# A triangular inverse from blocks of 4 instead of 16, and its last doubling applied to the right hand side

## The chip, the cores and the metric

The kernel runs on one core of one Trainium2 chip. The metric is the device time of one execution in microseconds (us). The engines named here are TensorE (PE, matmul; PEld is its weight load), VectorE (DVE), ScalarE (ACT), GpSimd (POOL) and SyncE (SP, which only issues DMAs here). Each works through its own instructions in order and waits for others on semaphores.

## The reference

Three model blocks run one after the other on a sequence of 1024 positions, width 1024, in fp32. The change concerns one part of the second block, a recurrence with 8 heads of 64 channels:

```python
def step(S, inp):
    r_t, w_t, k_t, v_t, a_t, b_t = inp
    sa = jnp.einsum('bhvk,bhk->bhv', S, a_t)
    S = S * w_t[:, :, None, :] + sa[..., :, None] * b_t[:, :, None, :] + v_t[..., :, None] * k_t[:, :, None, :]
    y = jnp.einsum('bhvk,bhk->bhv', S, r_t)
    return S, y
```

Its output is normalised over each head's 64 channels (mean, variance), scaled, given a bonus term and multiplied with a gate.

## The kernel before, in words

The recurrence is computed in 8 chunks of 128 positions (t = 0 to 7). Within a chunk the rank one updates depend on each other through a strictly triangular 128x128 matrix N for each head; the kernel builds X, the inverse of I minus N, and multiplies the right hand side with it. The 8 heads are handled as two groups b = 0, 1 of four (128x512 tiles, one 128x128 block c for each head).

A chunk is 22 steps on TensorE (`STEPS`, `step`). A step is 8 matmuls, four into one PSUM bank for each b; banks alternate with the step, so step j needs the bank that step j - 2 wrote to be emptied. Steps 0 to 4 are the scores (`SCORES`): D, Nt, Nk, Rb, Rk, products of features over 64 rows. VectorE masks them out of PSUM (`vector_step`); step 0's mask keeps what lies within blocks of 16, step 1 gives both Dt (VectorE) and the whole Nt (ScalarE). Steps 5 to 21 are the solve (`SOLVE`): inverses of blocks of 16 by powers (P2, P2t, P4, P4t, P8t and three additions X += ...), then three doublings to 32, 64 and 128, each a transpose Xt of X, a product Y of a masked part of N (M0, M1, M2) with X, and the addition X += Xt Y. ScalarE copies Xt and Y from PSUM, VectorE adds to X. GpSimd forms the initial X (`begin`) and M0 to M2 (`levels`).

When the inverse of chunk t - 1 is there, `right_side` (its right hand side, after step 21), `unknowns` (X times it, u), `outputs` (state update and y), `means` and `variances` follow, placed between the steps of chunk t. ScalarE takes the results (`take_right_side`, `take_unknowns`, `take_outputs`), VectorE updates the state (`renew`), centres and normalises y, ScalarE takes squares, Ln and Exp of the variance and applies the affine part (`affine`), GpSimd completes y with bonus and gate (`complete`).

In chunks 0 to 5 VectorE and ScalarE also prepare features for two chunks later (m = t + 2): `scale_now`, `shift` (six fused operations), `accumulate` (a scan), `keys`, `square`, `norms`, `clip`, `decays`, `logs`, `inverse_norms`, `directions`, `received`, `given`, `bonus_sums`, `give_bonus`. Chunks 6 and 7 have no m.

GpSimd spends the rest of its time on a convolution of 31 taps (two operations a tap, 128x1024 each); every fourth tap it does `complete(t - 2)`, `begin(t)` and `levels(t)`. Where each piece stands between the steps is written out by hand in the loops of `rwkv`.

Of the kernel before, what the change touches and what calls it, by code (L numbers as in the profile page):

```python
# [2238 lines left out]
STEPS = 22  # L2239


class ChannelParameters:
# [18 lines left out]
    def of(self, name):  # L2261
# [6 lines left out]
SOLVE = [("P2", "Dt", "D"), ("P2t", "D", "Dt"), ("X", "P2t", "X"),  # L2268
# [5 lines left out]

BY_VECTOR = {0: 1, 1: 2, 2: 3, 3: 4, 4: 5, 5: 6, 7: 7, 8: 8, 10: 9, 11: 10, 12: 11, 15: 12, 18: 13, 21: 14}
BY_SCALAR = {1: 1, 6: 2, 9: 3, 13: 4, 14: 5, 16: 6, 17: 7, 19: 8, 20: 9}
PER_VECTOR, PER_SCALAR = 14, 9

NEEDS = [(0, 0), (0, 0), (1, 0), (2, 1), (3, 0),
         (4, 0), (5, 0), (6, 2), (6, 2), (7, 2), (8, 3), (8, 3), (10, 3), (11, 3), (11, 3), (11, 5),  # L2280
         (12, 5), (12, 5), (12, 7), (13, 7), (13, 7), (13, 9)]


class Recurrence:


    def __init__(self, core, st, par, arena):
        sb = st.sb
        self.core, self.sig, self.par = core, st.sem, par
        self.mask = {n: sb(n, [P, P]) for n in ("mask_lt", "tri", "mask16", "mask16T", "level0", "level1", "level2")}  # L2290
# [9 lines left out]
        self.m = {n: tile(n) for n in ("D", "Dt", "Nt", "P2", "P2t", "Nk", "M0", "M1", "M2")}  # L2300
        self.m |= {"P4": self.m["D"], "P4t": self.m["Dt"], "P8t": self.m["P2t"], "Xt": self.m["Nt"], "Y": self.m["P2"]}
# [41 lines left out]
    def step(self, pe, t, j):  # L2343
# [4 lines left out]
        for b in range(2):  # L2348
            if j == 0 and t:
                self.after_scalar(pe, t - 1, b, 20)  # L2350
            if j == 1 and t:
                self.after_vector(pe, t - 1, b, 21)
# [5 lines left out]
            if j == 7:  # L2358
                pe.wait_ge(self.sig(f"begun{b}"), t + 1)
            if j == 14:  # L2360
                pe.wait_ge(self.sig(f"masked{b}"), t + 1)
        if j < 5:
            _, l, r = SCORES[j]
            for c in range(4):
                for b in range(2):
                    rows = slice(64 * b, 64 * b + 64)
                    mm = nc.tensor.matmul(core.acc[2 * b + j % 2][:, c * P:(c + 1) * P], self.chunk(l, t)[rows, c, :],
# [5 lines left out]
        for b in range(2):  # L2373
            for c in range(4):
                cs = slice(c * P, (c + 1) * P)
                to = core.acc[2 * b + j % 2][:, cs]
# [46 lines left out]

    def outputs(self, pe, t):
# [3 lines left out]
        pe.wait_ge(self.sig("u"), t + 1)  # L2428
# [50 lines left out]
    def scalar_step(self, a, t, j):  # L2479
# [3 lines left out]
        for b in range(2):  # L2483
# [321 lines left out]
def rwkv(core, par, x):  # L2805

    nc, d = core.nc, core.d
    with Stage(core, "rwkv") as st:
# [10 lines left out]
        with nc.Block() as block:  # L2819
# [66 lines left out]
            def _(pe):  # L2886
# [6 lines left out]
                for t in range(NT):  # L2893
# [3 lines left out]
                    for j in range(STEPS):  # L2897
# [5 lines left out]
                        if j == 3 and t:  # L2903
                            w.outputs(pe, t - 1)
# [1399 lines left out]
```

## Time and profile before

| | |
|---|---|
| median of 3 runs | 4715.8 us (4712.62 to 4719.29) |
| profiled execution, its own time | 4716.23 us |
| its span in the trace | 4714.5 us |
| TensorE busy | 4271.3 us (91%) |
| VectorE, ScalarE, GpSimd busy | 1893.1, 1342.0, 1140.6 us |
| one middle chunk, window 1743 to 1800 us: TensorE, VectorE, ScalarE, GpSimd busy | 50.66, 38.25, 27.76, 34.48 us |
| granted clock of the whole execution | 0.95 |

Times in the trace count from the start of the span. A timeline row gives the start, the duration of a run of equal instructions, the engine and line, what is written and read, how many there are, and in brackets the idle time before it and who ended it. Each fp32 matmul leaves two records, so a step of 8 matmuls is x16. A row's duration contains the drain of its last instruction; the distance of two starts is what a piece costs. Names drop indices: `rwkv_P_sb` is P2 or P4 or Y in the same buffer, `rwkv_Dt_sb` may hold P4t, `rwkv_Nt_sb` may hold Xt, `x_here` is the buffer that the features lie in.

### The profile page before, as it was taken

Reading aid. Unit: us, or ns where it says so; the run is one execution under the profiler, and the core shown is the slowest. Engines: PE = TensorE matmul, PEld = TensorE weight load, DVE = VectorE, ACT = ScalarE, POOL = GpSimd, SP = SyncE. Lnnn points to the kernel's source line nnn. Section 1 sums busy time; section 2 is a strip of 40 time slices with the busy share of each in tenths; the row PEclk is TensorE's granted clock in tenths of the full one; section 3 lists DMA queues with packets and bytes.
Section 4 is the critical chain, followed back from the end, with each engine's and each line's share of the span. In section 5 each row is a group of like instructions: output and inputs, shape, how many; then the busy total and the mean of one; then the engine's idle time right before and its main releaser. Section 6 shows DMA issues by size and latency. Waiting matters only on the chain. (4 is left out here: it accounts for less than half of the span.)

```text
span 4714.5 us, 55607 instructions
## 1 busy us (share of the span) xinstructions
PE 4271.3 (91%) x21558; PEld 3505.4 (74%) x21558; DVE 1893.1 (40%) x3298; ACT 1342.0 (28%) x2358; POOL 1140.6 (24%) x555
## 2 busy tenths in 40 slices
PE   8998797877996888689999999999999999977897
PEld 6887675766674888567888886888788888856676
DVE  3021565671487665255235334000033333346433
ACT  3120232341322444322000103112243444443112
POOL 2220001052152666222222221221111111122323
PEclk9998898978997999899999999999999999978899
DMA  3233101041442110121111112332333334266422
GB/s 123 101 143 91 33 17 43 22 139 45 156 148 97 39 41 19 51 100 45 45 54 45 49 41 78 121 135 86 104 94 92 93 109 109 61 208 191 163 78 92
DMA packets 279789, 413.05 MB, mean 88 GB/s; under 512 B 53109, under 2 KB 188150, under 8 KB 273658
## 3 DMA queue, kind: packets, MB, share of 16 engines
q1 hardware_dynamic: 224250, 310.02, 21.4%
q10 hardware_dynamic: 53104, 94.92, 5.4%
q0 software_dynamic: 2192, 4.80, 0.4%
q8 instruction: 162, 2.65, 0.2%
q14 instruction: 81, 0.66, 0.0%
HBM read 286.18 MB, written 123.47 MB: 87 GB/s over the span
## 5 line engine op out<-in xcount | busy, mean ns | idle before, releaser
L163 POOL TENSOR_TENSOR weights_wlow<-weights_raw,weights_whigh 128x1024 fp32r<-128x1024 f32 (+1 forms) x236 | 695.9, 2970 | 2444.5 <-ACT weights_whigh L154 2444.5
L154 ACT ACTIVATE weights_whigh<-weights_raw 128x1024 fp32r<-128x1024 f32 (+1 forms) x236 | 266.2, 1162 | 1176.5 <-PE acc L313 791.0
L313 PE MATMUL acc<-h_high_half,weights_whigh 128*128 128x512 f32 x1408 | 553.7, 393 | 25.0 <-POOL weights_wlow L163 21.2
L313 PE MATMUL acc<-h_high_half,weights_wlow 128*128 128x512 f32 x1408 | 550.4, 391 | 0.0
L313 PE MATMUL acc<-h_low_half,weights_whigh 128*128 128x512 f32 x1408 | 550.4, 391 | 0.0
L313 PEld LDWEIGHTS acc<-h_high_half,weights_whigh 128*128 128x128 f32 x1408 | 265.9, 189 | 89.8 <-POOL weights_wlow L163 22.5
L3524 PE MATMUL acc<-h_high_half,weights_whigh 128*128 128x512 f32 x768 | 331.3, 431 | 0.0
L313 PEld LDWEIGHTS acc<-h_low_half,weights_whigh 128*128 128x128 f32 x1408 | 265.9, 189 | 55.8
L313 PEld LDWEIGHTS acc<-h_high_half,weights_wlow 128*128 128x128 f32 x1408 | 265.9, 189 | 55.7 <-issue 1.0
L3524 PE MATMUL acc<-h_low_half,weights_whigh 128*128 128x512 f32 x768 | 302.2, 393 | 0.0
L3524 PE MATMUL acc<-h_high_half,weights_wlow 128*128 128x512 f32 x768 | 300.8, 392 | 0.0
L316 PE MATMUL acc<-weights_wlow,h_high_half 128*128 128x512 f32 x768 | 298.8, 389 | 0.0
L316 PE MATMUL acc<-weights_whigh,h_low_half 128*128 128x512 f32 x768 | 298.8, 389 | 0.0
L316 PE MATMUL acc<-weights_whigh,h_high_half 128*128 128x512 f32 x768 | 298.8, 389 | 0.0
L313 PE MATMUL acc<-y_high_half,weights_whigh 128*128 128x512 f32 x448 | 182.5, 407 | 30.4 <-DVE x_here L4087 19.8
L1972 DVE TENSOR_TENSOR x_here<-x_here,acc 128x512 f32<-128x512 f32 x80 | 54.9, 687 | 371.8 <-PE acc L313 371.8
L313 PE MATMUL acc<-hidden_high,weights_wlow 128*128 128x512 f32 x512 | 199.2, 389 | 0.0
L313 PE MATMUL acc<-hidden_high,weights_whigh 128*128 128x512 f32 x512 | 199.2, 389 | 0.0
L3432 DVE SCALAR_TENSOR_TENSOR gated_biased_sb<-gated_near_ends_sb,gated_slope_sb,acc 128x384 f32<-128x384 f32 x40 | 24.5, 614 | 413.2 <-DMA gated_end_sb<-rows 271.8
L313 PE MATMUL acc<-y_high_half,weights_wlow 128*128 128x512 f32 x448 | 179.6, 401 | 0.0
L313 PE MATMUL acc<-y_low_half,weights_whigh 128*128 128x512 f32 x448 | 179.3, 400 | 0.0
L3524 PEld LDWEIGHTS acc<-h_high_half,weights_whigh 128*128 128x128 f32 x768 | 145.8, 190 | 31.1
(536 smaller groups left out, 8174.2 us busy)
## 6 DMA issues: line engine op xcount, KB each, us to landing
weights_raw<-w_cols SPq DMA_DIRECT2D x94, 512.0 KB, 5.0
weights_raw<-w_ff SPq DMA_DIRECT2D x64, 512.0 KB, 3.8
weights_raw<-w_rows SPq DMA_DIRECT2D x30, 1024.0 KB, 7.1
att<-gated_result_sb SPq DMA_DIRECT2D x96, 130.0 KB, 2.2
merge_o_sb<-att SPq DMA_DIRECT2D x24, 520.0 KB, 6.7
rows<-norm_square ACTq DMA_DIRECT2D x48, 256.0 KB, 2.1
weights_raw<-w_out SPq DMA_DIRECT2D x24, 512.0 KB, 3.8
cols<-first_out ACTq DMA_DIRECT2D x40, 256.0 KB, 2.0
```

The source lines that it names most:

```text
L154: self.core.nc.scalar.activation(high[p][:, half * (KC // 2):(half + 1) * (KC // 2), :], raw[half], ACT.Copy).then_inc(self.core.sem("roun ...
L163: self.core.nc.gpsimd.tensor_tensor(low[p][:, hs, :], raw[half], high[p][:, hs, :].bitcast(F32), ALU.subtract).then_inc(self.core.sem("wei ...
L313: mm = nc.tensor.matmul(core.acc[b][:, :], wt[p][:, k, c * P:(c + 1) * P], h[:, k, half * HALF:(half + 1) * HALF], start=first, stop=final)
L316: mm = nc.tensor.matmul(core.acc[b][:, 0:width], h[:, k, b * P:(b + 1) * P], wt[p][:, k, :], start=first, stop=final)
L1972: return core.nc.vector.tensor_tensor(to, to, acc, ALU.add)
L3432: nc.vector.scalar_tensor_tensor(out=biased, in0=mask, scalar=self.slope[p][:, st["dilation"]:st["dilation"] + 1], in1=acc, op0=ALU.mult, ...
L3524: mm = nc.tensor.matmul(core.acc[b][:, :], wt[n % 2][:, k, c * P:(c + 1) * P], of[:, k, half * HALF:(half + 1) * HALF], start=(k == 0 and ...
```

## The change

Blocks of 4 are inverted by powers, which needs one square only (P2t) and one addition. Four doublings follow in place of three, to 8, 16, 32 and 64. So X holds the inverses of the two 64x64 diagonal blocks. The last doubling is applied to the right hand side: u's first half is X times the first 64 rows, a product with the off-diagonal block (`across`, copied out of step 0's bank by VectorE) is added to the second 64 rows (`raise_second`), and `unknowns` runs a second time for u's second half. Steps become 19. The order of the surrounding pieces on each engine changes too: `outputs` stand behind step 9 instead of 3, `means` behind 12, `variances` behind 15, `bonus_sums` behind 17; ScalarE has Ln and root of the variance apart from those of the norms, behind step 17; `levels` has a fourth mask M3 that waits for step 6.

```diff
-STEPS = 22
+STEPS = 19
-SOLVE = [("P2", "Dt", "D"), ("P2t", "D", "Dt"), ("X", "P2t", "X"),
-         ("P4", "P2t", "P2"), ("P4t", "P2", "P2t"), ("X", "P4t", "X"),
-         ("P8t", "P4", "P4t"), ("X", "P8t", "X"),
-         ("Xt", None, "X"), ("Y", "M0", "X"), ("X", "Xt", "Y"),
-         ("Xt", None, "X"), ("Y", "M1", "X"), ("X", "Xt", "Y"),
-         ("Xt", None, "X"), ("Y", "M2", "X"), ("X", "Xt", "Y")]
+SOLVE = [("P2t", "D", "Dt"), ("X", "P2t", "X")] + [
+    step for i in range(4) for step in (("Xt", None, "X"), ("Y", f"M{i}", "X"), ("X", "Xt", "Y"))]
...
-    def unknowns(self, pe, t):
+    def unknowns(self, pe, t, i):
-        pe.wait_ge(self.sig("rhs"), t + 1)
-        for b in range(2):
-            self.after_vector(pe, t, b, 21)
+        if i:
+            pe.wait_ge(self.sig("second"), t + 1)
+        else:
+            pe.wait_ge(self.sig("rhs"), t + 1)
+            for b in range(2):
+                self.after_vector(pe, t, b, 18)
...
+    def second_half(self, pe, t):
+
+        nc, core = self.core.nc, self.core
+        across = self.across[t % 2][:, :, :].rearrange("p i t -> p (i t)")
+        pe.wait_ge(self.sig("u"), 2 * t + 1)
+        for c in range(4):
+            for b in range(2):
+                e = slice(c * P + b * HD, c * P + (b + 1) * HD)
+                at = 4 * b + c
+                mm = nc.tensor.matmul(core.acc[4][:, e], across[:, at * HD:(at + 2) * HD], self.u[0:HD, e],
+                                      start=True, stop=True)
+        mm.then_inc(self.sig("second_sum"), 1)
...
+                if j == 0:
+                    ins.then_inc(self.sig(f"by_vector{b}"), 1)
+                    ins = nc.vector.tensor_copy(self.across[t % 2][:, 1 + 4 * b:5 + 4 * b, :], self.four(acc)[0:HD, :, HD:])
...
+    def raise_second(self, v, t):
+
+        second = self.rhs[HD:, :]
+        v.wait_ge(self.sig("rhs"), t + 1)
+        v.wait_ge(self.sig("second_sum"), t + 1)
+        self.core.nc.vector.tensor_tensor(second, second, self.core.acc[4][HD:, :], ALU.add).then_inc(self.sig("second"), 1)
...
+        for i in range(4):
+            for b in range(2):
+                if i == 0:
+                    self.after_scalar(pool, t, b, 1)
+                if i == 3:
+                    pool.wait_ge(self.sig(f"step{b}"), STEPS * t + 7)
...
                         w.step(pe, t, j)
                         if j == 1 and t:
-                            w.unknowns(pe, t - 1)
+                            w.unknowns(pe, t - 1, 0)
                         if j == 2:
                             w.turn(pe, t, 0)
                         if j == 3 and t:
-                            w.outputs(pe, t - 1)
+                            w.second_half(pe, t - 1)
...
                         if j == 6 and t:
+                            w.unknowns(pe, t - 1, 1)
+                        if j == 9 and t:
+                            w.outputs(pe, t - 1)
+                        if j == 12 and t:
                             w.means(pe, t - 1)
-                        if j == 8 and t:
+                        if j == 15 and t:
                             w.variances(pe, t - 1)
-                        if j == 18 and m:
+                        if j == 17 and m:
                             w.bonus_sums(pe, m)
                 w.right_side(pe, NT - 1)
-                w.unknowns(pe, NT - 1)
+                w.unknowns(pe, NT - 1, 0)
+                w.second_half(pe, NT - 1)
+                w.unknowns(pe, NT - 1, 1)
                 w.outputs(pe, NT - 1)
```

On TensorE, in front of the solve of a middle chunk, before: the last two products of `outputs`, score 4, a turn, step 5, a turn, the norms:

```order
3646 L2439 MATMUL acc<-rwkv_Rb_1_sb,rwkv_rhs_sb 64x128
3647 L2440 MATMUL acc<-rwkv_Rk_1_sb,rwkv_rows_sb 64x128
3648 L2367 MATMUL acc<-x_here 128x128 x8
3649 L2394 MATMUL acc<-ident_here,x_here 128x128 x4
3650 L2380 MATMUL acc<-rwkv_D_sb,rwkv_Dt_sb 128x128 x8
3651 L2394 MATMUL acc<-ident_here,rwkv_V_sb 128x128 x4
3652 L2452 MATMUL acc<-rwkv_sq_sb,rwkv_block_mean_sb 128x256 x2
```

The same place after the change, from score 3 to step 6 and the start of the second pass of the unknowns:

```order
3616 L2367 MATMUL acc<-x_here 128x128 x8
3617 L2436 MATMUL acc<-rwkv_rhs_sb,rwkv_across_sb 128x64 x8
3618 L2367 MATMUL acc<-x_here 128x128 x8
3619 L2394 MATMUL acc<-ident_here,x_here 128x128 x4
3620 L2380 MATMUL acc<-rwkv_Dt_sb,rwkv_D_sb 128x128 x8
3621 L2394 MATMUL acc<-ident_here,rwkv_V_sb 128x128 x4
3622 L2468 MATMUL acc<-rwkv_sq_sb,rwkv_block_mean_sb 128x256 x2
3623 L2380 MATMUL acc<-rwkv_X_0_sb,rwkv_P2t_sb 128x128 x4
3624 L2380 MATMUL acc<-rwkv_X_1_sb,rwkv_P2t_sb 128x128 x4
3625 L2424 MATMUL acc<-rwkv_rhs_sb,rwkv_X_0_sb 128x64
```

The 28 matmuls of `outputs` have left the place ahead of score 4 and eight products with across stand there.

On VectorE, the start of a middle chunk after the change (before it, the two masks D stood together and there was no copy to across):

```order
1238 L2620 TENSOR_TENSOR rwkv_D_sb<-acc,rwkv_mask_sb 128x512
1239 L2623 COPY rwkv_across_sb<-acc 64x256
1240 L2620 TENSOR_TENSOR rwkv_D_sb<-acc,rwkv_mask_sb 128x512
1241 L2623 COPY rwkv_across_sb<-acc 64x256
1242 L2620 TENSOR_TENSOR rwkv_Dt_sb<-acc,rwkv_mask4T_sb 128x512 x2
```

The rest of the chunk's front has the same operations in the same order up to Rk; behind it stands `raise_second`, ahead of the key product.

On ScalarE, the end of a chunk after the change: the last copies of Xt and Y, then what leads to the right side of the chunk:

```order
702 L2503 ACTIVATE rwkv_Dt_sb<-acc 128x512 x2
703 L2503 ACTIVATE rwkv_D_sb<-acc 128x512 x2
704 L2587 ACT_TABLE_LOAD
705 L2587 ACTIVATE rwkv_ysq_sb<-acc,rwkv_eps_sb 128x512
706 L2592 ACT_TABLE_LOAD
707 L2592 ACTIVATE rwkv_ysq_sb<-rwkv_ysq_sb 128x512
708 L2605 ACTIVATE rwkv_y_sb<-rwkv_y_sb,channel_parameters 128x128 x4
709 L2513 ACTIVATE rwkv_rhs_sb<-acc 128x512
```

Before, the copy of the right side (L2499) came directly behind the last copies of Y (L2489), and Ln, root and affine stood earlier in the chunk.

## Rows read from the trace of the kernel before

**Rows 1.** Timeline, TensorE: start, duration, line, operands; chunks 1, 4, 6, 7 start.

```profile
1571.60 2.06 PE L2367 MATMUL acc<-x_here 64*128 64x128 f32 x32
...
1742.30 2.06 PE L2367 MATMUL acc<-x_here 64*128 64x128 f32 x32
...
1856.10 2.06 PE L2367 MATMUL acc<-x_here 64*128 64x128 f32 x32
...
1911.77 2.06 PE L2367 MATMUL acc<-x_here 64*128 64x128 f32 x32
```

**Rows 2.** Timeline, TensorE, chunk 4 from the outputs on.

```profile
1748.98 0.49 PE L2431 MATMUL acc<-rwkv_rhs_sb,rwkv_rows_sb 128*128 128x128 f32 x2
...
1754.82 1.16 PE L2367 MATMUL acc<-x_here 64*128 64x128 f32 x16
...
1756.69 2.02 PE L2380 MATMUL acc<-rwkv_D_sb,rwkv_Dt_sb 128*128 128x128 f32 x16
...
1759.85 1.95 PE L2380 MATMUL acc<-rwkv_Dt_sb,rwkv_D_sb 128*128 128x128 f32 x16
...
1777.72 1.06 PE L2378 MATMUL acc<-ident_here,rwkv_X_sb 128*128 128x128 f32 x8 [0.98 <-DVE rwkv_X_sb L2611]
1778.62 1.95 PE L2380 MATMUL acc<-rwkv_X_sb,rwkv_M_sb 128*128 128x128 f32 x16
1781.35 2.02 PE L2380 MATMUL acc<-rwkv_P_sb,rwkv_Nt_sb 128*128 128x128 f32 x16 [0.78 <-ACT rwkv_P_sb L2489]
1784.35 1.06 PE L2378 MATMUL acc<-ident_here,rwkv_X_sb 128*128 128x128 f32 x8 [0.98 <-DVE rwkv_X_sb L2611]
```

**Rows 3.** Timeline, VectorE, the first half of chunk 4.

```profile
1743.49 1.29 DVE L2605 TENSOR_TENSOR rwkv_D_sb<-acc,rwkv_mask_sb 128x512 f32<-128x512 f32 x2 [3.03 <-PE acc L2367]
...
1749.81 1.27 DVE L2605 TENSOR_TENSOR rwkv_Nk_sb<-acc,rwkv_mask_lt_sb 128x512 f32<-128x512 f32 x2
...
1755.27 1.27 DVE L2605 TENSOR_TENSOR rwkv_Rb_sb<-acc,rwkv_tri_sb 128x512 f32<-128x512 f32 x2
...
1759.06 1.87 DVE L2660 TENSOR_TENSOR rwkv_kx_sb<-rwkv_kx_sb,rwkv_k_sb 128x512 f32<-128x512 f32 x1
...
1767.21 0.84 DVE L2624 TENSOR_TENSOR rwkv_S_sb<-rwkv_S_sb,acc 64x256 f32<-64x256 f32 x2
```

**Rows 4.** Timeline, GpSimd, the level masks of chunk 4.

```profile
1746.72 8.34 POOL L2746 TENSOR_TENSOR rwkv_M_sb<-rwkv_Nt_sb,rwkv_level_sb 128x512 f32<-128x512 f32 x6
```

**Rows 5.** Timeline, TensorE, the front of chunk 0.

```profile
1522.86 2.08 PE L2367 MATMUL acc<-x_here 64*128 64x128 f32 x16 [3.21 <-DVE rwkv_Nk_sb L2605]
...
1528.31 2.74 PE L2380 MATMUL acc<-rwkv_D_sb,rwkv_Dt_sb 128*128 128x128 f32 x16 [2.32 <-DVE rwkv_Rb_sb L2605]
...
1533.12 1.95 PE L2380 MATMUL acc<-rwkv_Dt_sb,rwkv_D_sb 128*128 128x128 f32 x16
```

**Rows 6.** Window of chunk 0: us, TensorE busy (records), granted clock, DMA share, GB/s.

```profile
1530.00:1531.00 1.00, 1.00 (x6) 0.50 0.00 0
```

**Rows 7.** Timeline, ScalarE: a decay in chunk 4; Ln, root, affine in the tail.

```profile
1764.15 0.39 ACT L2553 ACTIVATE rwkv_up_sb<-rwkv_C_sb,rwkv_middle_sb 128x128 f32<-128x128 f32 x1
...
1982.17 0.69 ACT L2572 ACTIVATE rwkv_ysq_sb<-acc,rwkv_eps_sb 128x512 f32<-128x512 f32 x1 [0.87 <-PE acc L2474]
1982.88 1.28 ACT L2577 ACT_TABLE_LOAD   x1
...
1985.56 1.65 ACT L2590 ACTIVATE rwkv_y_sb<-rwkv_y_sb,channel_parameters 128x128 f32<-128x128 f32 x4 [0.76 <-DVE rwkv_y_sb L2730]
```

**Rows 8.** Timeline, TensorE: last X step and start of the last outputs.

```profile
1962.86 2.02 PE L2380 MATMUL acc<-rwkv_P_sb,rwkv_Nt_sb 128*128 128x128 f32 x16 [0.78 <-ACT rwkv_P_sb L2489]
...
1970.88 0.49 PE L2431 MATMUL acc<-rwkv_rhs_sb,rwkv_rows_sb 128*128 128x128 f32 x2 [0.69 <-ACT rwkv_rhs_sb L2504]
```

**Rows 9.** Timeline, GpSimd and VectorE in chunk 0.

```profile
1530.89 2.85 POOL L2865 TENSOR_SCALAR rwkv_term_sb<-rwkv_conv_in_sb,rwkv_ctaps_sb 128x1024 f32<-128x1024 f32 x1
...
1532.11 0.67 DVE L2660 TENSOR_TENSOR rwkv_kx_sb<-rwkv_kx_sb,rwkv_k_sb 128x512 f32<-128x512 f32 x1
```

More of the change, by code:

```diff
@@ L2289, in __init__ @@
         self.core, self.sig, self.par = core, st.sem, par
-        self.mask = {n: sb(n, [P, P]) for n in ("mask_lt", "tri", "mask16", "mask16T", "level0", "level1", "level2")}
+        self.mask = {n: sb(n, [P, P]) for n in ("mask_lt", "tri", "mask4", "mask4T", "level0", "level1", "level2", "level3")}
         self.block_mean, self.keep = sb("block_mean", [P, P]), sb("keep", [P, 2 * QUARTER])
@@ L2299, in __init__ @@
         tile = lambda n: [sb(f"{n}{b}", [P, RW]) for b in range(2)]
-        self.m = {n: tile(n) for n in ("D", "Dt", "Nt", "P2", "P2t", "Nk", "M0", "M1", "M2")}
-        self.m |= {"P4": self.m["D"], "P4t": self.m["Dt"], "P8t": self.m["P2t"], "Xt": self.m["Nt"], "Y": self.m["P2"]}
+        self.m = {n: tile(n) for n in ("D", "Dt", "Nt", "P2t", "Nk", "M0", "M1", "M2")}
+        self.m |= {"Xt": self.m["Dt"], "Y": self.m["D"], "M3": self.m["P2t"]}
+        self.across = [sb(f"across{p}", [HD, 9, HD]) for p in range(2)]
         self.late = {n: [tile(f"{n}{p}_") for p in range(2)] for n in ("Rb", "Rk", "X")}
@@ L2366, in step @@
                     rows = slice(64 * b, 64 * b + 64)
-                    mm = nc.tensor.matmul(core.acc[2 * b + j % 2][:, c * P:(c + 1) * P], self.chunk(l, t)[rows, c, :],
+                    mm = nc.tensor.matmul(self.bank(t, j, b)[:, c * P:(c + 1) * P], self.chunk(l, t)[rows, c, :],
                                           self.chunk(r, t)[rows, c, :], start=True, stop=True)
@@ L2375, in step @@
                 cs = slice(c * P, (c + 1) * P)
[L2376 removed]
+                to = self.bank(t, j, b)[:, cs]
                 if l is None:
@@ L2741, in levels @@
     def levels(self, pool, t):
-        for b in range(2):
-            self.after_scalar(pool, t, b, 1)
-            for i in range(3):
-                ins = self.core.nc.gpsimd.tensor_tensor(self.four(self.tile(f"M{i}", t, b)), self.four(self.tile("Nt", t, b)),
-                                                        self.spread(self.mask[f"level{i}"]), ALU.mult)
-            ins.then_inc(self.sig(f"masked{b}"), 1)
+        for i in range(4):
[4 more added lines that the diff above has]
+                    pool.wait_ge(self.sig(f"step{b}"), STEPS * t + 7)
+                self.core.nc.gpsimd.tensor_tensor(self.four(self.tile(f"M{i}", t, b)), self.four(self.tile("Nt", t, b)),
+                                                  self.spread(self.mask[f"level{i}"]), ALU.mult).then_inc(self.sig(f"begun{b}"), 1)
     def complete(self, pool, f):
@@ L2967, in _ @@
                             w.take_rows(a, t, 2)
-                        if j == 7:
-                            if t:
-                                w.centre_squares(a, t - 1)
-                            if m:
-                                w.decays(a, m, 0)
+                        if j == 6 and t:
+                            w.take_unknowns(a, t - 1, 1)
+                        if j == 7 and m:
+                            w.decays(a, m, 0)
                         if j == 8 and m:
                             w.decays(a, m, 1)
-                        if j == 10:
+                        if j == 9:
                             if m:
                                 w.logs(a, m)
-                            if t:
-                                w.log_variance(a, t - 1)
-                            if m:
                                 w.inverse_norms(a, m)
-                            if t:
-                                w.root(a, t - 1)
+                        if j == 10 and t:
+                            w.take_outputs(a, t - 1)
+                        if j == 14 and t:
+                            w.centre_squares(a, t - 1)
+                        if j == 17 and t:
+                            w.log_variance(a, t - 1)
+                            w.root(a, t - 1)
                         if j == 18 and t:
@@ L2999, in _ @@
                 nc.vector.memset(w.eps[:, :], 64e-5)
+                for p in range(2):
+                    nc.vector.memset(w.across[p][:, 0, :], 0.0)
                 nc.vector.memset(w.S[:, :, :], 0.0).then_inc(sig("state"), 1)
```

97 lines of the change are left out of this document (49 added, 48 removed).

## The prediction, made before the changed kernel ran

> **What bounds the kernel now.** The windows of the page show TensorE as the busy engine everywhere, so the question is what sets the time of one stage, the recurrence (1513 to 1990 us). It works through 8 chunks, and the starts of a chunk on TensorE give its period [rows 1]: 56.90 us for each of the middle chunks 1 to 5 (two of them lie between 1742.30 and 1856.10), 55.67 for chunk 6, and chunk 1 starts at 1571.60. I call the time since a chunk's first score its place. TensorE is in order and nearly full: in a middle chunk it waits seven times, always in the solve, for 0.78 us (a ScalarE copy) or 0.98 us (a VectorE add or copy), 6.1 us in all [rows 2]. What is easily missed is the second engine. From place 1.2 (1743.49) to place 18.6 (1759.06 plus 1.87) VectorE does not pause: masks, six fused shifts, a scan, key product [rows 3]. The second three shifts fill 4.26 us from the end of the two Nk masks (1749.81 plus 1.20) to Rb (1755.27), 1.42 each, as long as one of GpSimd's six mask operations beside them (8.34 for six, 1.39 each): one shift gets in behind each of them [rows 3, 4]. TensorE has 5.84 us of outputs between scores 3 and 4 (1748.98 to 1754.82) and arrives at step 5 (1756.69) just as the mask Rb is done (1755.27 plus 1.27), so VectorE costs nothing there.
>
> **Part 1, the solve.** Four full product steps go (P2, P4, P4t, P8t); two of three power additions go too, and one doubling (transpose, Y, X) comes. A step is 1.86 us without a wait, a transpose 0.90 (1777.72 to 1778.62), from Y to X it is 2.73 (1.95 work, 0.78 wait), from X to the next transpose 3.0 [rows 2]. Work: 22 steps with 14 products in the solve become 19 with 10, so -4 x 1.86 + 0.90 = -6.5 us a chunk.
>
> **Part 2, the split right side.** Each chunk adds a second pass of 8 unknown products and 8 products with across. Neither is short for having 64 columns or 64 rows: weights of 128 columns are loaded for each, and all across products use the same 64 rows, so I take a step's 1.9 us for each, bounds 1.16 (the score at 1754.82, which runs its two row halves together) and 2.0 [rows 2]. Together +3.8. In the loop these passes lie in waits of others; TensorE pays their work only.
>
> **Part 3, VectorE in front.** Two copies of 64x256 are new before Dt. The nearest row is the state addition, 0.84 for two [rows 3]: +0.8 us. Outputs leave the place between scores 3 and 4; only the across products (1.9) stand there. Now TensorE is early. By places: scores 0, 1 and the first unknowns to 4.1, score 2, turn, score 3 to 6.9, across to 8.8; score 4 needs Nk, done at 8.8 now (1749.81 plus 1.27) and at 9.6 with the copies, hence 11.4 with the turn. Step 5 needs Rb, done at 14.2 now [rows 3] and at 15.0 then. GpSimd starts its masks some 2 us later than today, as it now completes an older chunk's output at the chunk's start; each shift still meets one of its operations, and I take the shifts at today's 1.42. **TensorE waits some 3.8 us there.** Step 5, a turn and the norms, 3.16 us now (1756.69 to 1759.85), put step 6 at 18.3 [rows 2].
>
> **Part 4, fillers.** Unknowns, outputs, means, variances now stand behind X steps and bonus behind Y, and use up the 0.98 and 0.78 waits (with a filler of 0.9 an X step still takes 3.0). At step 9 a price appears: ScalarE has half of the decays, four operations of 0.39 and two small ones that overlap [rows 7], between the copy of the transpose and that of Y: +0.6 us. Adding up from step 6 at 18.3: unknowns to 22.1, transpose and Y to step 9 at 26.4, outputs to 34.1, three doublings (0.9 + 2.73 + 3.0 twice, the last one 0.9 + 2.8 + 1.86) to 52.9, right side 2.7: period 55.6 at full clock, **1.3 us less than now**. Chunk 1 has no older chunk to complete, so GpSimd lets VectorE go earlier: 1.2 more.
>
> **Part 5, the clock.** Chunk 0 shows what a wait in front does: TensorE waits 3.21 us for Nk, then 2.32 for Rb, the granted clock falls to 0.50, the 1.2 GHz level, and step 5 to step 6 takes 4.81 us (1528.31 to 1533.12) where the full clock takes 3.16 [rows 2, 5, 6]. A wait of 3.8 us in every middle chunk should do the same: +1.6 us each, bounds 0 (the clock holds) and 2.8 (scores and step 6 too). Middle chunks: 5 x 1.3 + 1.2 - 5 x 1.6 = -0.3 us gained. So the recurrence gets nothing where VectorE has its preparation to do.
>
> **Part 6, chunks without preparation (6 and 7) and chunk 0.** Here VectorE has no shifts. Places: score 4 at 8.7, step 5 at 10.4, step 6 at 13.1, unknowns, transposes at 16.9, step 9 at 20.5 (no decays), outputs to 28.3, step 18 at 45.1 to 47.0, right side: 49.7. Against 55.67 that is 5.95 each, **11.9 us**. Chunk 0 has no unknowns and keeps its front: the shifts end with GpSimd's operations, so the 0.8 of copies is absorbed and step 5 stays at 1528.3. Afterwards 6 at 1533.1, 9 at 40.4, 12 at 47.4 (table loads delay two copies), 18 at 61.0, next chunk at 1565.6: **6.0 us**.
>
> **Part 7, the tail.** Nothing covers the split solve after the last chunk. Before, the last X step starts at 1962.86, ends at 1964.72, and outputs start 6.16 us later [rows 8]. After, ScalarE still has the previous chunk's Ln, root and affine in its queue before it takes the right side: load 1.28, Ln 0.7, load 1.28, and up to the affine's end 3.05 more (1984.16 to 1987.21), 6.3 us behind the last Y copy [rows 7]. The right side is then taken at 4.85 behind the X step, unknowns 2.0, half copy 0.65, across 2.0, addition 0.8, unknowns 2.0, copy 0.7: outputs at 13.05, **-6.9 us**, and 0.7 for the chance that the 2.2 us wait lowers the clock.
>
> **Sum.** 6.0 - 0.3 + 11.9 - 7.6 = 10.0 us off the profiled execution's 4716.2 (span 4714.5 plus 1.7), which is 0.4 above the median: 4705.8. The following stages wait for the end of this one, and take the gain whole.
>
> **GpSimd** needs a word of its own: one more level mask is two operations of 1.39 [rows 4], and its wait for step 6 adds idle time; busy 34.5 us of a chunk today, it will be busy some 37 of 55.6 or 49.7; the last mask M3 is ready by place 22, needed at 48. Nobody waits for it.
>
> **Rivals.** *The clock holds* (the wait is under 3.8, or split otherwise): the 8.0 and the 0.7 come back, 18.7 us, 4697.1. For it: the seven short waits of today leave the clock at 1.00. Against: chunk 0's 2.32 was enough. 17%.
>
> *The front is worse than laid out* (a shift misses a gap of GpSimd, 1.4 us, or the clock stays down to 2.8): 1 to 1.4 us more in each of 5 chunks, 3 to 5 us gained in all, 4711 to 4713. 17%.
>
> *GpSimd holds VectorE up in the middle, slower than before.* Directions, rates, renewal and the received features move into places 31 to 38, while GpSimd works on the taps; today these six run behind the taps. Should each wait for a GpSimd operation, the group takes 2 x 1.42 + 4 x 1.87 = 10.3 us instead of 6 x 0.67 = 4.0 at most, step 12's addition starts at 42.2 instead of 38.8, and the given features cost 1 more: 4.5 in 6 chunks, 27 us, so 4733. It decides once the group exceeds the roughly 7 us between inverse norms (31.3) and that addition. Against it: a key product took 0.67 in chunk 0 at 1532.11 in the middle of a GpSimd tensor_scalar (1530.89, 2.85 long), while one behind a GpSimd tensor_tensor took 1.87 [rows 9]. Only one tap operation in two holds it back, and the slack takes that. 8%. The Trainium skill (SBUF — State Buffer, section "Who interferes with whom") states that a VectorE instruction with two SBUF inputs contends with any GpSimd instruction that reads SBUF; by that rule the time would be this rival's, and the row at 1532.11 speaks against it.
>
> **How the numbers follow.** Forecast 58% (own range 4701 to 4711: across products at 1.1 give 5 more, clock cost 0.8 to 2.4 gives 4 either way). Range 4696 to 4715: it takes in the clock that holds and most of the worse front, and leaves out the slower rival. About 0.2%, 9.4 us, is what a measurement of this kernel tells from no change, and the forecast lies at that edge: faster by over 0.2% takes 0.17 and just over half of 0.58, 0.50; slower 0.08; the rest, 0.42, within.
>
> **What would show it.** Periods in the profile after: near 57 for chunks 2 to 5, 50 for 6, 52.6 for 0. A TensorE wait for Rb of 3 to 4 us per middle chunk, a granted clock below 1.00 behind it, shifts of 1.4 as today. Outputs 13 us behind the last X step. A middle period under 55 says the clock or the front was misread; a wait of step 13 or 16 for X over 1.5 us says it is GpSimd. A changed time outside the stage would make all of it wrong.

## The result, and the profile after

The changed kernel takes 4685.3 us (median; 4683.4 to 4691.9), the kernel before 4715.2 in the same comparison: a ratio of 0.9938, 95% interval 0.9921 to 0.9956, so 29.9 us less. The forecast was 4705.8 with a range down to 4696. The sign is right, the gain is three times what I gave, and the time lies outside the range. The profiled execution of after is the longest of its four (4691.9, span 4690.2), the others lie 6.5 to 8.5 us lower; the first experiment bears on why.

The stage by chunk, windows of the profiled execution, each from one first score matmul to the next, the last up to 1933. Columns: window and length, then busy time (records) of PE, PEld, DVE, ACT and POOL, the granted clock, DMA share, GB/s.

```profile
1512.50:1568.50 56.00, 40.71 (x318) 37.50 (x317) 34.40 (x44) 23.29 (x47) 35.61 (x19) 0.88 0.20 59
1568.50:1626.06 57.56, 48.69 (x426) 43.95 (x425) 38.19 (x50) 29.98 (x57) 34.80 (x18) 0.97 0.12 36
1626.06:1683.58 57.52, 48.78 (x426) 43.83 (x425) 39.78 (x51) 31.50 (x61) 37.57 (x20) 0.97 0.15 42
1683.58:1733.68 50.10, 46.64 (x425) 42.22 (x424) 32.98 (x51) 31.38 (x61) 40.91 (x20) 1.00 0.17 49
1733.68:1783.80 50.12, 46.66 (x426) 42.23 (x425) 33.01 (x51) 31.39 (x61) 40.91 (x20) 1.00 0.08 22
...
1833.91:1883.11 49.20, 45.25 (x418) 40.90 (x417) 18.22 (x30) 21.20 (x37) 35.47 (x20) 1.00 0.08 22
```

Before, every middle chunk took 56.90 [rows 1]. After, there are two kinds of them and nothing between: chunks 1 and 2 take 57.5, chunks 3, 4 and 5 take 50.1. The work is the same (425 or 426 matmul records in each). VectorE is busy 39.8 in one and 33.0 in the other, and GpSimd, the other way round, 37.6 and 40.9. I call them **held** and **free** chunks, after what happens to VectorE.

TensorE in a held chunk (2) and in a free one (4), in the timeline: start, us, engine, line, operation; in brackets the idle time before it and who ended it. First step 5 and step 6 of chunk 2:

```profile
1640.40 2.53 PE L2380 MATMUL acc<-rwkv_Dt_sb,rwkv_D_sb 128*128 128x128 f32 x16 [3.70 <-DVE rwkv_Rb_sb L2620]
1645.23 1.95 PE L2380 MATMUL acc<-rwkv_X_sb,rwkv_P2t_sb 128*128 128x128 f32 x16
```

and of chunk 4, with the product Y of step 9:

```profile
1743.72 1.95 PE L2380 MATMUL acc<-rwkv_Dt_sb,rwkv_D_sb 128*128 128x128 f32 x16
...
1746.81 1.95 PE L2380 MATMUL acc<-rwkv_X_sb,rwkv_P2t_sb 128*128 128x128 f32 x16
...
1754.69 2.02 PE L2380 MATMUL acc<-rwkv_D_sb,rwkv_Dt_sb 128*128 128x128 f32 x16 [1.54 <-ACT rwkv_D_sb L2503]
```

The held chunk is the one I forecast: 3.70 us of waiting for Rb (3.8 in Part 3), then step 5 to step 6 in 4.83 instead of 3.09, at a granted clock of 0.50 between 1642 and 1645, of which one window (columns as above):

```profile
1643.00:1644.00 1.00, 1.00 (x5) 0.92 (x4) 0.97 (x3) 0.75 (x2) 0.00 (x0) 0.50 0.00 0
```

The free chunk has no wait for Rb at all; step 6 stands at place 13.1 instead of 19.2. The cause stands on VectorE, here again chunk 2 and then chunk 4:

```profile
1630.31 0.47 DVE L2661 SCALAR_TENSOR_TENSOR rwkv_r_sb<-rwkv_raw_sb,channel_parameters,rwkv_r_sb 128x256 f32<-128x256 f32 x1
1630.70 1.49 DVE L2661 SCALAR_TENSOR_TENSOR rwkv_k_sb<-rwkv_raw_sb,channel_parameters,rwkv_k_sb 128x256 f32<-128x256 f32 x1
...
1738.34 0.47 DVE L2661 SCALAR_TENSOR_TENSOR rwkv_k_sb<-rwkv_raw_sb,channel_parameters,rwkv_k_sb 128x256 f32<-128x256 f32 x1
1738.73 0.47 DVE L2661 SCALAR_TENSOR_TENSOR rwkv_V_sb<-rwkv_raw_sb,channel_parameters,rwkv_V_sb 128x256 f32<-128x256 f32 x1
```

and on GpSimd, chunk 2 and chunk 4 (the initial X, two operations):

```profile
1630.37 2.96 POOL L2761 TENSOR_TENSOR rwkv_X_sb<-rwkv_D_sb,ident_here 128x512 f32<-128x512 f32 x2
...
1737.98 4.75 POOL L2761 TENSOR_TENSOR rwkv_X_sb<-rwkv_D_sb,ident_here 128x512 f32<-128x512 f32 x2
```

From the second shift on, a shift takes 0.47 us in the free chunk and 1.49 in the held one; in the free chunk it is GpSimd that needs 4.75 us for its two operations, which take 2.51 in chunk 1:

```profile
1570.46 2.51 POOL L2761 TENSOR_TENSOR rwkv_X_sb<-rwkv_D_sb,ident_here 128x512 f32<-128x512 f32 x2 [11.47 <-DVE rwkv_D_sb L2620]
```

In both chunks the first shift starts at place 4.25, ahead of GpSimd's operation, and takes 0.47; GpSimd's operation comes 0.06 us later in the held chunk and 0.04 in the free one. So the chunks part not at the first shift but at the second. Before, GpSimd's initial X was under way when the first shift came, in each chunk (in chunk 4 from place 1.96 to 4.47, the shift at 3.59). After, from chunk 2 on, it completes an older output first, at the start of the chunk, and the two meet.

The tail: ScalarE, then the three passes of the split solve and the outputs on TensorE.

```profile
1932.26 1.66 ACT L2605 ACTIVATE rwkv_y_sb<-rwkv_y_sb,channel_parameters 128x128 f32<-128x128 f32 x4 [0.76 <-DVE rwkv_y_sb L2753]
1933.82 0.57 ACT L2513 ACTIVATE rwkv_rhs_sb<-acc 128x512 f32<-128x512 f32 x1
```

```profile
1927.69 2.02 PE L2380 MATMUL acc<-rwkv_D_sb,rwkv_Dt_sb 128*128 128x128 f32 x16 [0.78 <-ACT rwkv_D_sb L2503]
1934.44 2.93 PE L2424 MATMUL acc<-rwkv_rhs_sb,rwkv_X_sb 128*128 128x64 f32 x16 [2.10 <-ACT rwkv_rhs_sb L2513]
1938.05 3.67 PE L2436 MATMUL acc<-rwkv_rhs_sb,rwkv_across_sb 64*128 64x64 f32 x16 [0.68 <-ACT rwkv_rhs_sb L2519]
1942.58 3.68 PE L2424 MATMUL acc<-rwkv_rhs_sb,rwkv_X_sb 128*128 128x64 f32 x16 [0.85 <-DVE rwkv_rhs_sb L2637]
1946.93 0.80 PE L2447 MATMUL acc<-rwkv_rhs_sb,rwkv_rows_sb 128*128 128x128 f32 x2 [0.68 <-ACT rwkv_rhs_sb L2519]
```

The last output is stored at 1967.95 where it was 1989.91. **Where the 21.96 us of the stage come from**, chunk by chunk against before: start 0.43; chunk 0 58.64 - 55.97 = 2.67; chunks 1 and 2 -0.66 and -0.62; chunks 3 to 5 6.8 each, 20.4; chunk 6 6.47; chunk 7 with the tail 78.14 - 84.84 = -6.70. Another 2.3 of the span's 24.3 lie in later stages, spread over many waits; single executions of the kernel before differ by more (4712.6 to 4719.3).

### The profile page after: what moved, and what is told of

Read it like the earlier page. It is cut to its first block and busy times, and to the rows that moved or that the text cites. A ratio compares the mean times of both kernels' runs of the same rounds, so it can differ in the third digit from the quotient of the medians.

```text
span 4690.2 us, 55196 instructions
## 1 busy us (share of the span) xinstructions
PE 4257.3 (91%) x21366; PEld 3493.4 (74%) x21366; DVE 1868.5 (40%) x3260; ACT 1366.5 (29%) x2392; POOL 1172.8 (25%) x571
```

## The experiments

All edits are to the changed kernel unless said. The starts of the chunks in each profiled execution give the periods that the verdicts rest on; for the overview first the table, worked out from the first score matmul of each chunk in the timelines (no chunk follows chunk 7; "7 + tail" is from its start to the next stage's load of the finished rows):

| kernel | ch 0 | 1 | 2 | 3 | 4 | 5 | 6 | 7 + tail |
|---|---|---|---|---|---|---|---|---|
| before | 58.6 | 56.9 | 56.9 | 56.9 | 56.9 | 56.9 | 55.7 | 84.6 |
| after | 56.0 | 57.6 | 57.5 | 50.1 | 50.1 | 50.1 | 49.2 | 91.3 |
| after, once more | 56.4 | 57.5 | 50.1 | 50.2 | 50.1 | 50.1 | 49.2 | 91.1 |
| GpSimd behind all six shifts | 46.1 | 51.2 | 51.2 | 51.2 | 51.1 | 51.2 | 49.2 | 91.6 |
| GpSimd ahead of the shifts | 56.2 | 57.5 | 57.6 | 57.6 | 57.6 | 58.4 | 49.2 | 91.3 |
| before, GpSimd behind the shifts | 52.3 | 56.5 | 56.5 | 56.5 | 56.5 | 56.6 | 55.7 | 83.6 |
| GpSimd behind the first shift | 52.2 | 56.9 | 50.1 | 50.1 | 50.1 | 50.1 | 49.2 | 90.1 |
| and the tail's order | 46.1 | 51.2 | 51.2 | 51.2 | 51.2 | 51.2 | 49.2 | 87.1 |
| and decays earlier | 45.8 | 51.2 | 51.2 | 51.2 | 51.2 | 51.2 | 49.2 | 91.3 |
| and unsplit | 53.9 | 57.3 | 58.8 | 57.3 | 58.8 | 57.4 | 56.9 | 83.0 |
| and unsplit, logarithm later | 54.1 | 55.7 | 55.9 | 55.9 | 55.9 | 55.9 | 53.7 | 86.3 |
| all that helped | 45.8 | 49.7 | 49.7 | 49.7 | 49.7 | 49.7 | 49.2 | 88.8 |

The lines that begin with "and" are edits on top of "GpSimd behind all six shifts".

**The same kernel once more.**

> The kernel after, unchanged. Theory A (a race for the memory port): whether a middle chunk has a period of 50.1 or 57.5 us is decided by which of two operations starts first at place 4.3, the first shift on VectorE or GpSimd's initial X, and they lie 0.04 to 0.06 us apart. So the number of chunks with 50.1 differs from one execution to the next, with no period in between, and the times lie in steps of about 7.4 us: 4684.6 (one slow chunk less than in the profile) or 4691.9. Rival B (the first chunks are slow for a reason of their own, such as the loads still under way): chunks 1 and 2 are slow and 3 to 5 fast in every execution.

4683.8 us (4680.9 to 4690.0, 4 runs), ratio 0.9927 [0.9911, 0.9944]. Chunk 2, held in the first profile, is free in this one. Windows of chunks 1 and 2, columns as above:

```profile
1568.89:1626.41 57.52, 48.66 (x425) 43.99 (x424) 38.19 (x50) 29.82 (x57) 34.78 (x18) 0.97 0.12 36
1626.41:1676.50 50.09, 46.66 (x425) 42.23 (x424) 33.03 (x51) 31.34 (x61) 40.91 (x20) 1.00 0.17 48
```

and GpSimd's initial X of that chunk, whose first shift starts at 1630.67:

```profile
1630.70 4.75 POOL L2761 TENSOR_TENSOR rwkv_X_sb<-rwkv_D_sb,ident_here 128x512 f32<-128x512 f32 x2
```

It comes 0.03 us behind the shift here, 0.06 in the first profile. Theory A holds for chunk 2 in what matters, same program, same chunk, 7.4 us apart, with no period between; its wording does not, since the first shift starts ahead of GpSimd in both. Rival B keeps a part: chunk 1 is held in both, for a steady reason. It has no older output to complete, so GpSimd starts its initial X at 1570.46 in the first profile, well ahead of the first shift (1572.76). The executions of after, 4691.9 and 4690.0 on one side, 4680.9 to 4685.4 on the other, fit one chunk more or less being held, though only two of them have a profile.

**GpSimd's initial X behind the shifts.** In `begin`, for chunks 0 to 5:

```diff
+        if t + 2 < PAIRS:
+            pool.wait_ge(self.sig("shifted"), 6 * (t + 2) + 6)
         for b in range(2):
             pool.wait_ge(self.sig(f"by_vector{b}"), PER_VECTOR * t + 1)
```

> One wait more on GpSimd: the initial X of chunks 0 to 5 starts only when the six shifts are done. Theory A: the shifts take 0.47 us each in every chunk, chunks 1 to 5 all have periods of 50.1 us, the waits for Nk and Rb in chunk 0 (2.65 and 2.33) go with their clock loss: 4691.9 - 2 x 7.4 - about 6 = 4671 us. Rival B: the order on GpSimd is without effect, chunks 1 and 2 stay at 57.5, 4685 us.

4672.9 us (4668.5 to 4674.0), ratio 0.990 [0.9883, 0.9916]: 11 less than after measured beside it, by a wait and nothing else. Chunk by chunk against the second run of after, chunk 0 gives 10.3 and chunk 1 gives 6.4, the two in which GpSimd was always first; chunks 2 to 5, free in that run, lose 1.0 to 1.1 each. All 36 shifts take 0.46 or 0.47. Chunk 0 loses 10 us rather than the 6 expected, since with the front its 3.16 us wait for X ahead of step 13 and the half clock behind that (step 14 took 3.57) go too. The middle chunks come out at 51.2, not 50.1: GpSimd's work now runs later, and VectorE's group in the middle of the chunk is slower (in chunk 4 the directions take 2.42 us for two and the state's fade 2.73, against 1.45 and 1.72 in the free chunk 4 of after). TensorE waits 1.17 for X ahead of step 13, where a free chunk has no wait. TensorE in chunk 3, the Y of step 9 and the transpose of step 13:

```profile
1681.69 2.02 PE L2380 MATMUL acc<-rwkv_D_sb,rwkv_Dt_sb 128*128 128x128 f32 x16 [1.53 <-ACT rwkv_D_sb L2503]
...
1696.99 1.07 PE L2378 MATMUL acc<-ident_here,rwkv_X_sb 128*128 128x128 f32 x8 [1.17 <-DVE rwkv_X_sb L2629]
```

**GpSimd first.** `w.begin` stands ahead of `w.complete` in GpSimd's loop.

> On GpSimd the initial X stands ahead of the two operations that complete an older output, as it did before at place 2. Theory A: GpSimd is always at work when the first shift comes, the shifts take 1.4 to 1.5 us in all of chunks 0 to 5, every middle period is 57 to 58 us, TensorE waits 3.7 us for Rb, clock 0.50 behind it: 4691.9 + 3 x 7.4 = 4714 us. Rival B: 4685 us, chunks 3 to 5 at 50.

4717.4 us (4714.2 to 4721.6, 10 runs), ratio 0.9998 [0.9988, 1.0007]. Every middle chunk is held, and the whole gain is gone. Chunk 3, window and TensorE's wait ahead of step 5:

```profile
1685.25:1742.80 57.55, 48.76 (x426) 43.93 (x425) 39.84 (x51) 31.45 (x61) 37.37 (x20) 0.97 0.15 42
```

```profile
1699.62 2.92 PE L2380 MATMUL acc<-rwkv_Dt_sb,rwkv_D_sb 128*128 128x128 f32 x16 [3.71 <-DVE rwkv_Rb_sb L2620]
```

The period is close to what the prediction adds up to, 55.6 plus 1.6 for the clock (chunk 5 alone took 58.4). So this kernel is nearest to the one I forecast, except that its tail, chunk 0 and chunk 1 are dearer than I had them.

**The kernel before, with the same wait on GpSimd.**

> The kernel before with the same wait on GpSimd (initial X only behind the six shifts). Theory A: VectorE's front shortens by some 5 us here too, but the outputs between scores 3 and 4 keep TensorE busy until then, so chunks 1 to 5 stay at 56.9 us; only chunk 0, which has no outputs, loses its waits of 3.2 and 2.3 us and 1.6 of clock: 4708 us. If instead the middle periods of the kernel before fall too, VectorE's front bounded that kernel as well. Rival B: 4715 us.

4709.9 us (4702.6 to 4711.6, 10 runs), ratio 0.9978 [0.9969, 0.9988]: 9 us less. Chunk 0 gives 6.4, the middle chunks 0.36 each. With the outputs between scores 3 and 4 a faster front brings the old kernel next to nothing in the loop. The shifts take 0.47 to 0.48 there too, so it is the new order of the fillers that makes the front count, and the free shifts that make it short.

**Behind the first shift only.** The same wait with `+ 1` instead of `+ 6`.

> GpSimd's initial X waits only for the first of the six shifts instead of all six. Theory A1 (who is first keeps the port: VectorE's operations that follow one another without a pause hold GpSimd off until a mask comes that reads PSUM): the shifts stay at 0.47, GpSimd's two operations of the initial X slip into the masks, as in the fast chunks of the kernel after, all middle periods 50.1 instead of 51.17 us of the kernel with the full wait, 4672.9 - 5.3 = 4667.6 us. Rival A2 (the order of starting matters only because GpSimd idles; as soon as it is let in, it holds the later shifts): the second three shifts take 1.4 to 1.5, periods 54 to 57.5, 4690 to 4704 us.

4681.6 us (4679.7 to 4682.1). Neither theory whole: four chunks are free at 50.1, chunk 1 is held at 56.9, chunk 0 takes 52.2. VectorE and GpSimd in chunk 1:

```profile
1570.11 0.47 DVE L2661 SCALAR_TENSOR_TENSOR rwkv_k_sb<-rwkv_raw_sb,channel_parameters,rwkv_k_sb 128x256 f32<-128x256 f32 x1
1570.51 1.49 DVE L2661 SCALAR_TENSOR_TENSOR rwkv_V_sb<-rwkv_raw_sb,channel_parameters,rwkv_V_sb 128x256 f32<-128x256 f32 x1
```

```profile
1570.27 3.11 POOL L2763 TENSOR_TENSOR rwkv_X_sb<-rwkv_D_sb,ident_here 128x512 f32<-128x512 f32 x2 [12.16 <-DVE rwkv_r_sb L2661]
```

GpSimd arrives 0.16 us behind the start of k, waits for k's end, and is let in before V. In chunk 2 it arrives at the same distance (k at 1627.00, GpSimd at 1627.16) and is held off through V, and so in chunks 3 to 5; in chunk 0, 0.22 behind k, it is let in before V. In these rows an operation that is under way keeps its pace; what happens at the boundary to the next one is not decided by the distance alone, and stays open. Of the two waits tried, only the full one frees the shifts in all chunks.

**The tail's order.** In the last chunk the affine step of chunk 6 moves behind `take_unknowns`:

```diff
-                        if j == 18 and t:
+                        if j == 18 and 0 < t < NT - 1:
                             w.affine(a, t - 1)
...
                 w.take_unknowns(a, NT - 1, 1)
+                w.affine(a, NT - 2)
```

> The kernel with the full wait on GpSimd, and in the last chunk ScalarE takes the right side and both halves of the unknowns ahead of the affine step of the chunk before. TensorE's wait of 2.09 us ahead of the last unknowns becomes 0.55. If the clock then stays at full speed, the three passes of the split solve take 2.0, 1.9 and 2.0 instead of 3.44, 3.67 and 3.68 and the outputs start at full speed: 1.5 + 5 + 1.9 = 8.4 us, 4664.5 us. If the clock falls all the same, only the 1.5 us: 4671.4 us.

4667.2 us (4666.4 to 4667.5), 5.7 less than without it, between the two cases. The two were measured in different comparisons; taken each against the kernel before beside it, the difference is 4.7 (50.7 and 46.0).

```profile
1912.29 2.00 PE L2424 MATMUL acc<-rwkv_rhs_sb,rwkv_X_sb 128*128 128x64 f32 x16 [0.69 <-ACT rwkv_rhs_sb L2513]
1914.97 2.00 PE L2436 MATMUL acc<-rwkv_rhs_sb,rwkv_across_sb 64*128 64x64 f32 x16 [0.68 <-ACT rwkv_rhs_sb L2519]
1917.82 3.68 PE L2424 MATMUL acc<-rwkv_rhs_sb,rwkv_X_sb 128*128 128x64 f32 x16 [0.85 <-DVE rwkv_rhs_sb L2637]
```

The wait shrinks by 1.40 (2.09 to 0.69), and two passes that took 3.44 and 3.67 take 2.00 each, 4.5 us together and the whole change of the tail (91.57 to 87.10). The third pass still runs at a clock of 0.50: three waits of 0.69, 0.68 and 0.85 us ahead of it went with that. When the clock falls is not settled by these waits: the last kernel below has the same tail, and there it is down already for the second pass, behind 0.69 and 0.68, and the tail takes 88.8.

**Decays earlier.** ScalarE's first half of the decays moves from step 7 to behind step 5.

> The kernel with the full wait on GpSimd, and the first half of the decays moved from between the transpose's copy and the Y copy (step 7) to the idle time of ScalarE behind step 5. If the price of the decays at step 9 is what the prediction said, TensorE's wait there falls from 1.53 (1.36 in chunk 0) to 0.78 us: 5 x 0.75 + 0.6 = 4.4 us, 4668.5 us. If ScalarE comes late with something else, or VectorE's later timetable bounds the chunk, nothing: 4673 us.

4672.7 us (4669.7 to 4677.7), no change against 4672.9, the periods likewise. TensorE's waits in chunk 3:

```profile
1679.55 2.02 PE L2380 MATMUL acc<-rwkv_D_sb,rwkv_Dt_sb 128*128 128x128 f32 x16 [0.78 <-ACT rwkv_D_sb L2503]
...
1695.63 1.06 PE L2378 MATMUL acc<-ident_here,rwkv_X_sb 128*128 128x128 f32 x8 [1.95 <-DVE rwkv_X_sb L2629]
```

The wait at step 9 went from 1.53 to 0.78 (the prediction priced it at 0.6), and the wait at step 13 from 1.17 to 1.95 took it all back. The wait is for VectorE's addition to X, which stands behind its group of directions, rates, renewal and received features; the last experiment moves that group.

**Without the split.** Five level masks, five doublings (22 steps), the full inverse, one pass of unknowns, no copies of the across block.

> The kernel with the full wait on GpSimd, and the last doubling as a matrix step again: five level masks, five doublings, 22 steps, no copies of the across block, no second half, one pass of unknowns. By the prediction's terms a doubling costs 6.6 us and the split 3.8, so 2.8 more in chunks 1 to 7 and 6.6 more in chunk 0; the tail's outputs start 6.2 instead of 17.9 us behind the last X step: 7 x 2.8 + 6.6 - 11.7 = +14.5, 4687.4 us, with middle periods of 54.0. If the split passes cost less than I took (1.2 each), 5 to 10 us more than that.

4718.9 us (4710.1 to 4722.6, 10 runs), 46 more, three times what I expected. Part of that was my placement: ScalarE's Ln and root, with their table loads, stood in front of the last doubling's copies, and TensorE waited 2.42 there.

> The unsplit kernel once more, with the logarithm, root and affine of the older chunk placed behind the copies of the last doubling instead of in front of them, which cost a wait of 2.42 where others are 0.78 and a fall of the clock in every second chunk (periods 57.3 and 58.8). Expected: periods of chunks 1 to 5 57.3 - 1.6 = 55.7, chunk 7's tail as in the first unsplit kernel, 4718.9 - 7 x 1.6 - 3 x 1.5 = 4703 us. That would put the price of a doubling as a matrix over the split at 55.7 - 51.2 = 4.5 us a chunk in the loop, against 2.8 by the prediction's terms; if it comes to 54.0 the prediction's terms hold.

4703.6 us (4697.7 to 4706.8, 7 runs), ratio 0.9971 [0.996, 0.9982]. With that mended the middle period is 55.9. Against the split at 51.2 the matrix doubling costs 4.7 us a chunk, 4.5 in chunk 6, 8.0 in chunk 0, and gives back 5.2 in chunk 7 with the tail. By the terms of Parts 1 and 2 it should be 2.8 (6.6 less 3.8) in the loop. The other 1.9 are for the most part waits that the split's passes cover: without them TensorE waits 0.64 for Rb, 0.49 for Rk and 0.98 for X behind step 6, 2.1 us, and the split kernel has none of the three. (The account is not exact: the split kernel in turn waits 1.17 at step 13, which this one does not.) In the loop the two passes cost some 1.9 (6.6 less 4.7), not 3.8. In all the split is worth 31 us with this order (4703.6 against 4672.9). The three waits in chunk 4 of the unsplit kernel:

```profile
1740.35 2.02 PE L2379 MATMUL acc<-rwkv_Dt_sb,rwkv_D_sb 128*128 128x128 f32 x16 [0.64 <-DVE rwkv_Rb_sb L2616]
1744.17 2.02 PE L2379 MATMUL acc<-rwkv_X_sb,rwkv_P2t_sb 128*128 128x128 f32 x16 [0.49 <-DVE rwkv_Rk_sb L2616]
1747.17 1.06 PE L2377 MATMUL acc<-ident_here,rwkv_X_sb 128*128 128x128 f32 x8 [0.98 <-DVE rwkv_X_sb L2622]
```

**All that helped in one.** The full wait on GpSimd, the tail's order, the decays, and on VectorE:

```diff
-                        if j == 11:
-                            if t:
-                                w.renew(v, t - 1)
-                            if m:
-                                w.received(v, m)
+                        if j == 10 and m:
+                            w.received(v, m)
...
+                        if j == 15 and t:
+                            w.renew(v, t - 1)
```

> All that helped in one: the full wait on GpSimd, the tail's order on ScalarE, the first half of the decays behind step 5, and on VectorE the received features right behind the directions, the given ones behind step 12 and the state's renewal behind step 15. If VectorE's group of directions, renewal and received features, 9.6 us long beside GpSimd's taps, is what took back the 0.75 us of the decays (a wait for X of 1.95 ahead of step 13), that wait goes and the middle period becomes 50.1 - 0.75 = 49.4 us: 4667.2 - 5 x 1.8 - 0.5 = 4657.7 us. If the wait only moves to step 16 or to the right side, 4664 to 4667 us.

4660.6 us (4659.8 to 4664.8), ratio 0.9878 [0.9861, 0.9894]. The wait at step 13 is gone and 0.43 us remain at step 16; middle chunks take 49.7, 0.3 more than expected. The tail gave less than in the kernel that brought its order (88.8 against 87.1), since the second pass ran at half clock here:

```profile
1907.36 3.67 PE L2436 MATMUL acc<-rwkv_rhs_sb,rwkv_across_sb 64*128 64x64 f32 x16 [0.68 <-ACT rwkv_rhs_sb L2519]
```

The window of chunk 3:

```profile
1656.62:1706.27 49.65, 46.65 (x425) 42.15 (x424) 35.17 (x51) 31.56 (x61) 37.77 (x20) 1.00 0.17 49
```

This version is 58 us faster than the kernel before beside it, against 35 for the change in the comparison of its second run, and all its middle chunks have one period in the one execution profiled.

## Why the prediction was wrong in size

**Part 3, "each shift still meets one of its operations, and I take the shifts at today's 1.42", is the step that failed** ("its" is GpSimd's). It held in chunks 1 and 2 and failed in 3 to 5. I had seen that GpSimd "starts its masks some 2 us later than today", and noted the work that it does first, but did not place that against the shifts. The masks of D and Dt and the copies end at place 4.2; the affine step is done at 1.7, the older output takes GpSimd 2.6 us, and it is free at 4.3. A tie to within 0.1 us has two outcomes, and I priced one. The price of the other: shifts of 0.47, no wait of 3.7, no fall of the clock, and no wait of 1.5 ahead of step 13, so 57.5 - 50.1 = 7.4 us a chunk, 6.0 of them ahead of step 6. Three free chunks are 22 us, more than the forecast's whole gain. The kernel with GpSimd first, where all are held, took the time of the kernel before; with GpSimd behind all six, every shift takes 0.47. How often the tie falls one way no sum of mine could have given: three of the four chunks that meet it were free in one execution and four of four in the other.

The Trainium skill (SBUF — State Buffer, section "Who interferes with whom") says that where VectorE and GpSimd contend for the port pair they share, the one that issues first has it for the whole instruction and the other is blocked (it says so of VectorE's 2-port modes), and that the order of issue decides who blocks. I had drawn on that section for the rule on which operations contend, and not for this one. The rows agree for a single operation: the first shift, under way when GpSimd comes, takes 0.47 in both kinds of chunk, and where GpSimd is let in the shift behind it takes 1.49. The masks, with one input in PSUM, take 1.27 for two in held and free chunks alike. But the order of the starts does not part the two kinds, for VectorE was first in both; what the rows add is that VectorE's operations in close succession can keep GpSimd out over three of them.

**Part 5, the clock: right where its condition held.** Held chunks measured 57.5 where 55.6 + 1.6 = 57.2 was forecast, with 4.83 us from step 5 to step 6 against the 4.81 that I took from chunk 0. That the period is so near is in part luck, two misses that nearly cancel. Step 6 stands at place 19.2 and not at 18.3 + 1.6 = 19.9, because the 0.8 us of the copies is absorbed (the last shift starts at place 11.52 in chunk 2, and at 11.56 in the middle chunks before): I had reasoned so for chunk 0 and not for these. And the rest of the chunk takes 38.4 instead of 37.3, with a wait of 1.48 ahead of step 13 that I did not have. The 1.2 for chunk 1 did not come either: its last shift starts at 11.56. The rival "the clock holds" described the free chunks' clock, for another reason.

**Parts 1, 2 and 4: right, as sums.** From step 6 to the next chunk I had 55.6 - 18.3 = 37.3 us; a free chunk takes 37.0. The wait at step 9 was to be 0.78 + 0.6, it is 1.54. Chunk 6 was to take 49.7 and takes 49.2. The unsplit kernel adds that leaving the two passes out saves less than their 3.8 us of work, because they cover waits that would stand there without them.

**Part 6, chunk 0: 2.7 us instead of 6.0.** The front is as forecast (step 6 at 1532.7, forecast 1533.1). Missing was a wait of 3.16 us for the X of step 12, ahead of step 13, and the half clock that follows it:

```profile
1552.04 1.06 PE L2378 MATMUL acc<-ident_here,rwkv_X_sb 128*128 128x128 f32 x8 [3.16 <-DVE rwkv_X_sb L2629]
1552.94 3.57 PE L2380 MATMUL acc<-rwkv_X_sb,rwkv_M_sb 128*128 128x128 f32 x16
```

Chunk 0 has no outputs, so its steps come earlier against the preparation. VectorE had directions, 3.07 for two (0.87 before), beside GpSimd's taps, and more of its group behind them when X was due:

```profile
1544.79 3.07 DVE L2698 SCALAR_TENSOR_TENSOR rwkv_kk_sb<-rwkv_k_sb,channel_parameters,rwkv_sq_sb 128x256 f32<-128x256 f32 x2 [2.18 <-ACT rwkv_sq_sb L2582]
```

That is the third rival, "GpSimd holds VectorE up in the middle", in one chunk of six; in the held chunks it adds a wait of 1.49 at step 13, in the free ones nothing. I gave it 8% as a case for all chunks, where it was to be a term.

**Part 7, the tail: 13.2 us instead of 7.6**, counted from the last X step to the store (27.05 before, 40.26 after). The waits were right: the right side is taken 4.27 behind the X step, forecast 4.85. The clock was not. I set 0.7 aside for it; that term is the one mis-sized here: three passes at 2.93, 3.67 and 3.68 instead of 2.0 each are 4.3, and the outputs (8.46 up to their copy instead of 5.97) another 2.5. The kernel with the tail's order puts the first wait of 2.1 us at 1.4 that could be saved of itself and 3.1 by the clock; in the last kernel, with the same order, the clock fell one pass earlier and only some 2.8 of these 4.5 came.

**Sum by the prediction's own terms:** forecast 10.0; free chunks +21.3 (3 x 7.1, against the forecast period of 57.2); chunk 0 -3.3; chunks 1 and 2 -1.9 (the 1.2 for chunk 1 did not come); chunk 6 +0.5; tail -5.6; chunk 7's own loop +0.6; start +0.4. That is 22.0, the stage's 21.96.

## What to carry to other kernels

Where VectorE and GpSimd both work out of SBUF, write down for each operation which one is under way when the other starts; where they start within a tenth or two of a microsecond, the time can have two values (50.1 and 57.5 us a chunk here). A semaphore on the less urgent engine takes the choice away. It is not free: the chunk takes 51.2 with it, not 50.1, and most of its 11 us came from the two chunks in which GpSimd had always been first. A program whose repeated stretches show two periods and nothing between may have such a tie. And when a filler that covered an engine's front is moved away, price that front in both orders, not at the duration it happened to have under cover.

## What the runs showed of the hardware

- A 128x256 scalar_tensor_tensor on VectorE took 0.47 us free and 1.49 behind a GpSimd tensor_tensor on 128x512; three in succession kept GpSimd off for 1.2 us. A GpSimd operation that arrived 0.03 to 0.05 us behind the first of them was kept off through all three (chunks 2 to 5 of the second run of after, chunks 3 to 5 of the first); one that arrived 0.06 behind it got in after the first (chunk 2 of the first run). With the wait for the first shift, one that arrived 0.15 to 0.16 behind the second got in after it in chunk 1 and was kept off in chunks 2 to 5. What the boundary depends on is open.
- The same program ran chunk 2 in 57.52 and in 50.09 us in two executions.
- In the tail the granted clock fell to 0.50 with no single wait above 0.85 us in the reordered kernel (0.69, 0.68, 0.85), and in the last kernel behind 0.69 and 0.68 alone. Middle chunks kept 1.00 with waits of 0.78, 1.53 and 1.17, or 0.78 and 1.95, spread over 51 us (GpSimd behind all six shifts; and decays earlier).
